# Experts' rooms by rank: 53 units of 128, 96, 64 and 32 places instead of 56 units

## The reference, cut to what matters

```python
def _moe(h, p):                                  # h: 384 x 1024
    ...                                          # top 8 of 64 experts for each token
    hg = jnp.einsum('td,edf->tef', h, p['w_gate'])      # 64 x 1024 x 128
    hu = jnp.einsum('td,edf->tef', h, p['w_up'])        # 64 x 1024 x 128
    act = jax.nn.silu(hg) * hu * gates[:, :, None].astype(h.dtype)
    routed = jnp.einsum('tef,efd->td', act, p['w_down'])   # 64 x 128 x 1024
    shared = (jax.nn.silu(h @ p['ws_gate']) * (h @ p['ws_up'])) @ p['ws_down']
    return routed + shared
```

## Time and profile before

| | |
|---|---|
| median of 3 runs | 1691.47 us (1687.89 to 1701.95) |
| profiled execution, its own time | 1706.42 us |
| its span, first to last instruction | 1704.6 us |
| PE busy | 1406.1 us, 82% of the span |
| DVE, ACT, POOL busy | 671.4, 408.3, 256.3 us |
| mean granted clock of PE | 0.881 of 2.4 GHz |
| moved by DMA | 378.96 MB, 222 GB/s over the span |
| chain that ended last | PE 71%, DVE 16%, DMA 6% |
| of it in the expert stage | L1143 25%, L1158 11%, L1129 7% |

### The profile page before, as it was taken

One profiled execution on the slowest core, in us unless ns is written; L12 is line 12 of the kernel. 1 busy time (PEld: TensorE's weight loads), 2 busy tenths in 40 slices (PEclk: granted clock), 3 DMA queues, 4 the chain that ended last, 5 costly groups with the idle time before them and its releaser, 6 DMA issues.

```text
span 1704.6 us, 23713 instructions
## 1 busy us (share of the span) xinstructions
PE 1406.1 (82%) x8772; PEld 962.6 (56%) x8772; DVE 671.4 (39%) x1382; ACT 408.3 (24%) x788; POOL 256.3 (15%) x273
## 2 busy tenths in 40 slices
PE   4799687986999999997059996888889999999942
PEld 2598465954555555554028875676655555555521
DVE  4422767153332222222743347633523222222246
ACT  2324425021222222221013344321112122222201
POOL 1000000001322222231010000000023232322200
PEclk9799857977999999999579996699889999999975
DMA  9553202126988888885874412122469888888853
GB/s 319 206 183 118 105 31 109 50 87 233 362 305 317 328 333 324 305 332 181 340 257 173 141 70 99 41 99 99 180 252 358 333 313 307 324 294 298 328 207 154
DMA packets 126098, 378.96 MB, mean 222 GB/s; under 512 B 28224, under 2 KB 33152, under 8 KB 122784
## 3 DMA queue, kind: packets, MB, share of 16 engines
q1 hardware_dynamic: 86976, 291.31, 46.2%
q0 software_dynamic: 35552, 60.97, 10.1%
q10 hardware_dynamic: 3456, 25.17, 3.6%
HBM read 480.36 MB, written 64.75 MB: 320 GB/s over the span
## 4 chain that ended last, share of the span: by engine, by line
PE 71%; DVE 16%; DMA 6%; issue 4%; ACT 2%; SPq 0%; DVEq 0%; ACTq 0%; POOLq 0%
PE bank L1143 25%; PE bank L1158 11%; PE bank L1129 7%; PE bank L1050 5%; PE bank L771 4%; PE bank L772 4%; PE bank L773 4%; DVE aT L1843 4%; DMA ring<-in_w_ada 3%; DVE aT L1580 1%; PE bank L1066 1%; DMA ring<-in_w_in 1%; PE bank L790 1%; PE bank L1114 1%; PE bank L976 1%
## 5 line engine op out<-in xcount | busy, mean ns | idle before, releaser
L1143 PE MATMUL bank<-slab,xT 128*64 128x256 f32 x2112 | 301.5, 396 | 20.6 <-issue 20.5
L1143 PEld LDWEIGHTS bank<-slab,xT 128*64 128x64 f32 x2112 | 180.6, 142 | 104.2 <-issue 38.2
L732 POOL DMA_INDIRECT sums_scratch<-h,row_table x112 | 112.8, 1007 | 538.6 <-PE bank L1129 438.4
L1826 DVE TENSOR_TENSOR work<-work,bank 128x128 f32<-128x128 f32 x112 | 32.3, 288 | 399.1 <-ACT work L1405 399.1
L1143 PE MATMUL bank<-ring,xT 128*64 128x256 f32 x960 | 152.7, 392 | 9.6 <-issue 9.6
L1158 PE MATMUL bank<-slab,work 128*64 128x512 f32 x528 | 147.3, 592 | 1.5 <-DVE work L1832 1.5
L1405 ACT ACTIVATE work<-bank 128x128 f32<-128x128 f32 x112 | 31.1, 278 | 457.5 <-PE bank L1143 457.5
L1815 DVE COPY h<-bank 128x512 f32<-128x512 f32 x112 | 77.5, 692 | 127.0 <-PE bank L1158 127.0
L1143 PEld LDWEIGHTS bank<-ring,xT 128*64 128x64 f32 x960 | 90.1, 140 | 44.8 <-issue 14.8
L1143 PE MATMUL bank<-h_hi_slot,xT 128*64 128x256 f32 x512 | 108.5, 396 | 6.4 <-issue 6.4
L1492 DVE TENSOR_TENSOR w_lo<-ring,w_hi 128x2048 fp32r<-128x2048 f32 x24 | 55.0, 2292 | 122.3 <-ACT w_hi L1229 122.3
(11 more groups left out here) (334 smaller groups left out, 2324.9 us busy)
## 6 DMA issues: line engine op xcount, KB each, us to landing
slab<-in_w_gate SPq DMA_DIRECT2D x112, 512.0 KB
slab<-in_w_up SPq DMA_DIRECT2D x112, 512.0 KB
slab<-in_w_down SPq DMA_DIRECT2D x112, 512.0 KB
ring<-in_w_ada SPq DMA_DIRECT2D x24, 2048.0 KB
ring<-in_w_gate SPq DMA_DIRECT2D x52, 512.0 KB
ring<-in_w_up SPq DMA_DIRECT2D x52, 512.0 KB
ring<-in_w_down SPq DMA_DIRECT2D x52, 512.0 KB
slab<-sums_scratch ACTq DMA_DIRECT2D x24, 1024.0 KB, 11.5
```

Source lines behind the costliest of these rows:

```text
L732: pool.indirect_dma_start(sums_dram, bass.IndirectOffsetOnAxis(ap=row_table[:, u:u + 1], axis=0), y_rows[:, n % 3, :], None, bounds_check= ...
L1143: last = mm(bk[r, 0:2 * P].rearrange("p (k f) -> p k f", k=2), xT[:, n % 2, j, r], w[:, j, :, :], start=(j == 0), stop=(j == NJ - 1))
```

## The change: rooms by rank, and products of the unit's own widths

There are 53 units. Ranks 0 to 7 have 128 places (8 units, kind "whole"); ranks 8 to 15 have 96, and share their unit with one of the ranks 56 to 63, which have 32 (8 units, "mixed"); ranks 16 to 47 have 64 (16 units, "pair"); ranks 48 to 55 have 32, four to a unit (2 units, "quad"); 19 units of two windows are spare. A turn is pair, whole, spare, pair, mixed, spare (the first: pair, whole, pair, mixed, spare, spare); turns 2 and 5 have a quad and a spare more, the last one a spare more.

A whole unit's products use 128 stationary columns, one product where two were. A mixed unit has three products of 64, 32 and 32 columns; a quad four of 32. The places and rooms come from a table by rank: constants that DVE builds at the start (`by_rank`), three products of it with a one-hot of the ranks (bank "rooms"), and a copy. The counts are divided into windows only after that, since the room is subtracted first. The 7 slots, L652 and the conditional loads stay as they are.

```diff
@@ -29,14 +29,15 @@
 BASE = 8
-LAYER_DVE = 159
+START_DVE = 29
+LAYER_DVE = 156
 NSLOT = 2
...
 WIN = 64
-NUNITS = 56
-WHOLE = 16
-PAIRED = 24
-NXW = 32
+NUNITS = 53
+BASE_UNITS = 34
+SPARE = NUNITS - BASE_UNITS
+NXW = 2 * SPARE
 EMPTY = 65536
...
@@ -46,6 +47,33 @@
               ("c_lat", 512), ("s_lat", 512), ("tie", 64))
+
+
+def windows_of(unit):
+
+    if unit < 8:
+        return [(0, P, unit)]
+    if unit < 16:
+        return [(0, 96, unit), (96, P, unit + 48)]
+    if unit < 32:
+        return [(0, WIN, unit), (WIN, P, unit + 16)]
+    if unit < BASE_UNITS:
+        return [(GROUP * k, GROUP * (k + 1), 48 + 2 * k + unit - 32) for k in range(4)]
+    return [(0, WIN, 64 + unit - BASE_UNITS), (WIN, P, 64 + unit - BASE_UNITS + SPARE)]
+
+
+def steps_by_rank(value, slope):
+    out = []
+    for r in range(1, len(value)):
+        if value[r] != value[r - 1] + slope:
+            out.append((r, value[r] - value[r - 1] - slope))
+    return out
+
+
+BY_RANK = sorted((r, unit * P + lo, hi - lo) for unit in range(BASE_UNITS) for lo, hi, r in windows_of(unit))
+PLACE_STEPS = steps_by_rank([place for _, place, _ in BY_RANK], P)
+ROOM_STEPS = steps_by_rank([room for _, _, room in BY_RANK], 0)
 
...
@@ -412,6 +444,7 @@
         banks.plan("layer", "ranks", 1, [7])
+        banks.plan("layer", "rooms", 1, [1])
         banks.plan("layer", "ysh", 2 * NTILE, [0, 1, 2, 3, 4, 5])
...
@@ -521,18 +554,22 @@
             landed.append(fix_sum[b % NSLOT])
-        UNITS_BY_KIND = {"whole": list(range(WHOLE)), "pair": list(range(WHOLE, WHOLE + PAIRED)),
-                         "spare": list(range(WHOLE + PAIRED, NUNITS))}
-        order_of_units = []
-        loads, loads_of_unit = [], []
+        UNITS_BY_KIND = {"whole": list(range(8)), "mixed": list(range(8, 16)), "pair": list(range(16, 32)),
+                         "quad": list(range(32, BASE_UNITS)), "spare": list(range(BASE_UNITS, NUNITS))}
+        order_of_units, loads, tiles_of_unit = [], [], []
         for turn in range(8):
-            for kind in ("pair", "whole", "pair", "spare", "pair", "whole", "spare"):
+            kinds = ("pair", "whole", "spare", "pair", "mixed", "spare") if turn > 0 else ("pair", "whole", "pair", "mixed", "spare", "spare")
+            for kind in kinds + {2: ("quad", "spare"), 5: ("quad", "spare"), 7: ("spare",)}.get(turn, ()):
                 u = UNITS_BY_KIND[kind].pop(0)
-                owners = {"whole": [u], "pair": [u, u + PAIRED], "spare": [E + u - WHOLE - PAIRED, E + u - WHOLE - PAIRED + 16]}[kind]
-                loads_of_unit.append([len(loads) + i for i in range(len(owners))] * (2 if kind == "whole" else 1))
-                loads += [(len(order_of_units), w) for w in owners]
+                tiles = []
+                for lo, hi, w in windows_of(u):
+                    cuts = [lo, 64, hi] if hi - lo == 96 else [lo, hi]
+                    tiles += [(slice(p, q), len(loads)) for p, q in zip(cuts, cuts[1:])]
+                    loads.append((len(order_of_units), w))
+                tiles_of_unit.append(tiles)
                 order_of_units.append(u)
-        assert sorted(order_of_units) == list(range(NUNITS)) and len(loads) == E + NXW
+        assert all(w < E for _, w in loads[:XSLOT])
+        assert sorted(order_of_units) == list(range(NUNITS)) and sorted(w for _, w in loads) == list(range(E + NXW))
 
...
@@ -1102,7 +1136,13 @@
                 banks.filled(mm(bk[:, 0:E], ones[0:E, :], is_less[0:E, :], start=True, stop=True), "ranks")
-                shared_up(1, range(2, NJ))
+                shared_up(1, range(2, 4))
+                bk = banks.claim(pe, "rooms")
+                banks.wait_emptied(pe, "ranks")
+                for k in range(3):
+                    last = mm(bk[:, k * E:(k + 1) * E], by_rank[:, k * P:(k + 1) * P], of_rank[0:E, :], start=True, stop=True)
+                banks.filled(last, "rooms")
+                shared_up(1, range(4, NJ))
                 bk = banks.claim(pe, "owner")
...
@@ -1130,16 +1170,15 @@
                 def up(n):
-                    for half in range(2):
-                        _, full, level = expert_slot(n, half)
+                    for i in sorted({i for _, i in tiles_of_unit[n]}):
+                        _, full, level = load_slot(i)
                         pe.wait_ge(full, level(l))
...
                     for j in range(NJ):
-                        for half in range(2):
-                            r = slice(WIN * half, WIN * (half + 1))
-                            w = expert_slot(n, half)[0][:, 0:2 * D].rearrange("p (k j f) -> p j k f", k=2, j=NJ)
+                        for r, i in tiles_of_unit[n]:
+                            w = load_slot(i)[0][:, 0:2 * D].rearrange("p (k j f) -> p j k f", k=2, j=NJ)
                             last = mm(bk[r, 0:2 * P].rearrange("p (k f) -> p k f", k=2), xT[:, n % 2, j, r], w[:, j, :, :],
...
@@ -1153,9 +1192,8 @@
                         bk = banks.claim(pe, stage, 0, n)
-                        for half in range(2):
-                            r = slice(WIN * half, WIN * (half + 1))
-                            last = mm(bk[r, :], actT[:, n % 2, r], expert_slot(n, half)[0][:, 2 * D + c * 512:2 * D + (c + 1) * 512],
+                        for r, i in tiles_of_unit[n]:
+                            last = mm(bk[r, :], actT[:, n % 2, r], load_slot(i)[0][:, 2 * D + c * 512:2 * D + (c + 1) * 512],
                                       start=True, stop=True)
...
@@ -1429,13 +1467,26 @@
             copy, red = nc.vector.tensor_copy, nc.vector.tensor_reduce
-            order = InOrder(dve, dve_order, 6, LAYER_DVE, DEPTH)
+            order = InOrder(dve, dve_order, START_DVE, LAYER_DVE, DEPTH)
             after = order.after
...
             dve.sem_inc(slots_idle.sem, 1)
+            dve.wait_ge(ids_ready, 1)
+            after(ts(rank_id[:, :], tie_col[:, :], -1.0, float(E - 1), ALU.mult, ALU.add))
+            ts(rank_col[:, 0:1], rank_id[:, :], float(P), None, ALU.mult)
+            after(nc.vector.memset(rank_col[:, 1:2], float(P)))
+            for k, steps in ((0, PLACE_STEPS), (1, ROOM_STEPS)):
+                for first, change in steps:
+                    after(ts(rank_step[:, :], rank_id[:, :], float(first), float(change), ALU.is_ge, ALU.mult))
+                    after(tt(rank_col[:, k:k + 1], rank_col[:, k:k + 1], rank_step[:, :], ALU.add))
+            after(tt(rank_col[:, 2:3], rank_col[:, 0:1], rank_col[:, 1:2], ALU.add))
+            after(ts(rank_col[:, 2:3], rank_col[:, 2:3], -1.0, float(BASE_UNITS * P), ALU.mult, ALU.add))
+            for k in range(3):
+                last = ts(by_rank[:, k * P:(k + 1) * P], ones[0:E, :], rank_col[:, k:k + 1], None, ALU.mult)
+            after(last)
             dve.wait_ge(consts_in, 16 * NCONST)
...
@@ -1729,38 +1780,33 @@
                 ts(is_less[0:E, :], key_row[0:E, :], key_col[0:E, :], None, ALU.is_lt).then_inc(less_ready.sem, 1)
-                copy(count_i, count)
-                after(ts(place_i[:, 0, :], loads_row, float(WIN - 1), None, ALU.add))
+
+                ranks = banks.read(dve, "ranks")
+                banks.emptied(ts(of_rank[0:E, :], ranks[0:E, 0:E], rank_id[:, :], None, ALU.is_equal), "ranks")
+                rooms = banks.read(dve, "rooms")
+                banks.emptied(copy(rstd[:, 2 * E:5 * E], rooms[:, 0:3 * E]), "rooms")
+                banks.wait_emptied(dve, "rooms")
+                tt(count_i, count, over_tiles_e(room), ALU.subtract)
+                after(stt(place_i[:, 0, :], loads_row, float(WIN - 1), room, ALU.add, ALU.subtract))
                 ts(count_i, count_i, 6, None, ALU.arith_shift_right)
...
                 copy(over_a[:, :, :], count_i)
-
-                ranks = banks.read(dve, "ranks")
-                after(ts(room, ranks[:, 0:E], float(WHOLE), None, ALU.is_lt))
-                ts(far, ranks[:, 0:E], float(WHOLE + PAIRED), float(WIN - PAIRED * P), ALU.is_ge, ALU.mult)
-                after(ts(room, room, 1.0, None, ALU.add))
-                banks.emptied(stt(own_place, ranks[:, 0:E], float(P), far, ALU.mult, ALU.add), "ranks")
-                after(tt(extra, place_i[:, 1, :], room, ALU.subtract))
-                after(ts(extra, extra, 0.0, None, ALU.max))
+                after(ts(extra, place_i[:, 1, :], 0.0, None, ALU.max))
                 after(nc.vector.tensor_tensor_scan(spans[:, 1, :], ones[:, 0:E], extra, 0.0, ALU.mult, ALU.add))
...
 
-                tt(over_base, spans[:, 0, :], room, ALU.subtract)
                 tt(own_span[0:E, :, :], spans[0:E, :, :], ident[0:E, 0:E].unsqueeze(1).broadcast_to([E, 2, E]), ALU.mult)
-                after(red(rank_col[0:E, :], is_less[0:E, :], AX.X, ALU.add))
+                after(red(rank_of[0:E, :], is_less[0:E, :], AX.X, ALU.add))
                 red(span_col[0:E, :], own_span[0:E, :, :], AX.X, ALU.add)
-                after(ts(rank_col[0:E, :], rank_col[0:E, :], -1.0, float(E - 1), ALU.mult, ALU.add))
```

(24 more changed lines are left out.)

## The result

| | before | after |
|---|---|---|
| median | 1693.8 us (4 runs) | 1908.8 us (4 runs, 1902.6 to 1915.2) |
| ratio | | 1.1266, 95% interval 1.1204 to 1.1328 |
| profiled execution, its span | 1706.4, 1704.6 us | 1907.8, 1906.0 us |
| expert stages, first to last unit's row | 378.6 and 382.1 us | 477.8 and 478.5 us |
| PE busy | 1406.1 us | 1509.3 us |

The account below looks back on a forecast made before the run. PE leads, busy over 95%, but not alone (DMA 83%), with waits for late weights. Stages +85.5 and routing +4.8 give +90.3 on the 1691.5 us median: 1782 us, range 1690 to 1895.

Parts of the forecast that it names:

- The step that failed: Products of mixed units: a 64-wide tile beside two 32-wide ones was taken to cost 0 us extra.
- The bound from above: Mixed units' up and down products, if both widths cannot run at once: 7.1 us more per unit.
- the sum: Whole kernel: +85.5 us in the expert stages and +4.8 us for routing, together +90.3 us.
- The rival's size: Mixed units' widths do not overlap: 56.8 us per layer, +46 after fewer waits, 1874 us in all; chance 0.27.
- The slots: Expert stages: order of loads against 7 slots makes weights late, 90 us of waits per layer; DMA share near 0.75.
- first pairs: First pairs of turns, units 6, 12, 26, 32, 46: last load's gate only three units earlier, late 2.2 us, five times.
- DMA volume: Rival for the expert stages: same bytes at share 0.83 take the same 380 us, 1696 us in all; chance 0.10.
- Three units less: Expert stages: three units go, at 6.456 us each, -19.4 us per layer.
- Routing: Ahead of the expert stage: DVE waits for small products, +2.7 less 0.3, +2.4 us per layer, +4.8 in all.
- Start: Kernel start: 26 new DVE operations end before 8 us while DVE idles until 13.48; 0 us.
- Full width: Whole units' products: one full-width product needs the same time as a pair; 0 us.
- Spare loads: Real spare windows in smaller rooms: one or two per layer possible, 0 to 5.3 us each; taken as 0.

Follow-up runs that it names:

- a_m32: Kernel after, with the 96-place window of each mixed unit cut into three 32-wide tiles, so all four tiles are 32 wide; 1801.4 us, ratio 1.0637.
- b_mix: Kernel before, with the second half of each of its 24 paired units cut into two 32-wide tiles beside the first half's 64; 2018.0 us.
- b_late: Kernel before, spare windows given a slot only when the unit three places ahead is through, real windows taking slots before; 1649.4 us, ratio 0.973.
- b_quart: Kernel before, with every paired unit done as four 32-wide tiles, loads and order untouched; 1696.6 us.
- a_halves: Kernel after, with whole units again done as two tiles of 64 columns; 1906.5 us.
- a_m32_late: Kernel after, mixed units in four 32-wide tiles, spare windows given slots only when the unit two places ahead is through; 1776.5 us.

## Why the prediction failed

- **The step that failed** is "Mixed units have a 64-wide tile beside two 32-wide ones, which no row shows ... I take 0, nearest to the two rows in which tiles do overlap". Both rows show tiles of one width. The bound from above was the truth: 7.1 us, measured 7.4 in the profile after (11.95 against 6.51 for unit 3, 8.55 against 6.59 for unit 5, after against a_m32) and 7.5 in b_mix. One step j of unit 10's up phase takes 1.13 us (496.67 to 497.80), where a step at one width takes 0.43 (794.34 to 794.77 in unit 55 of the kernel before). That is 2 x 0.43, the 64-wide tile and then the two 32-wide ones, and 0.27 more, about 0.14 for each of two changes of width, where I had taken 0.1. Two steps in the profile after, with the two 32-wide tiles of the first, which do run together (497.48 and 497.49), and one step of the kernel before:

```profile
496.67 0.98 PE L1182 MATMUL bank<-h_hi_slot,xT 128*64 128x256 f32 x3
497.48 0.38 PE L1182 MATMUL bank<-h_hi_slot,xT 128*32 128x256 f32 x1
497.49 0.38 PE L1182 MATMUL bank<-ring,xT 128*32 128x256 f32 x1
497.80 0.98 PE L1182 MATMUL bank<-h_hi_slot,xT 128*64 128x256 f32 x3
```

```profile
794.34 0.38 PE L1143 MATMUL bank<-slab,xT 128*64 128x256 f32 x1
...
794.77 0.38 PE L1143 MATMUL bank<-slab,xT 128*64 128x256 f32 x1
```

- The Trainium skill, TensorEngine Tiling (Array Packing), Tiling Modes, says that changing the tiling mode drains the engine, and lists 128x64 and 128x32 as different configurations. The trace agrees: 0 for four equal tiles in the up phase, 7.5 us for a mixture in b_mix.
- **What it weighs.** In spans the sum was 111.1 us short (201.4 against 90.3): 118.4 for 16 mixed units at 7.4, less 8.3, since the waits beside them were 85.5 and 86.2 us and not 90, and 1 for routing.
- **The rival's size.** With it I had 1874. In profiles it gives +182 against +201.4 measured. Of the difference, 5 us are 7.4 instead of 7.1, 12 are waits (I had taken 10.5 off 90.2 for each layer), about 1 is routing. Against the medians 13 us more are missing: the profiled execution of before ran 12.6 us over its median, those of the other kernels within 2, and I took its 55.7 us of waits for typical. Outside the stages it had 943.9 us, b_late 940.9 and b_quart 943.1, so most of the 13 us probably lay in the stages' own waits; no second trace of the kernel before shows it.
- **The slots: right**, in mechanism and size. Waits of 91.1 and 92.7 us in a_m32 for 90.2, and a DMA share of 0.74 and 0.72 for the 0.75 foretold. By kind, in its layer 0: unit 18 late by 14.3 (12.8 forecast), unit 20 by 10.6 (8.6), mixed units by 1.6 to 6.0, five of the seven by 4.2 or more (5.2), first pairs by 0.3 to 1.8 (2.2). That DMA volume isn't the limit is shown by b_late.
- **Three units less**: their 19.4 us per layer are in both sums. PE lost more in the eight mixtures, 59 us.
- **Routing: right.** From the ranks product to the maximum with zero there were 1.48 us (379.07 to 380.55 in the earlier trace rows); now 4.26. That is +2.8, forecast +2.7:

```profile
378.26 0.43 PE L1138 MATMUL bank<-norm_t,ones 64*128 64x64 f32 x2
...
380.11 0.88 PE L1143 MATMUL bank<-norm_t,by_rank 64*128 64x64 f32 x6
```

```profile
382.52 0.19 DVE L1794 TENSOR_SCALAR work<-work 128x64 f32<-128x64 int32 x1
```

- **Start: right.** The table is done at 6.3 us and DVE idles 7.37 us where it idled 12.43:

```profile
5.61 0.67 DVE L1488 TENSOR_SCALAR by_rank<-ones,rank_col 64x128 f32<-64x128 f32 x3
13.65 0.56 DVE L1491 CAST masks<-h 128x768 uint8<-128x768 f32 x1 [7.37 <-DMA lb_all<-in_lower_bounds]
```

- **Full width: right**, 0 (a_halves). **Spare loads: right** for the kernel after: one real window appeared, in layer 0, and its unit was in time.

## What to carry to other kernels

Rows of two tilings that each overlap say nothing about the two mixed: keep one tile width within a phase, even at the price of more products. A prefetch ring counts what is reserved, not what is fetched: give a slot to an optional transfer as late as its issue, done or not done, still lands in time, and check by walking the list which earlier unit each load waits for. When two resources are nearly in balance (64 loads of some 5.3 us, 340 us of DMA work, against 352 of PE here), the order of demands decides before either total does.

## What the runs showed of the hardware

Products 64 and 32 columns wide on different columns of the array run one after the other with about 0.14 us per change (1.13 us for a step of 2 x 0.43), while four of 32 or two of 64 run together: 64 products of 256 columns in 3.66 us, 32 in 3.67. A change of width between one unit and the next costs about as much: steps of 6.59 us in b_quart for 6.45. A conditional transfer that isn't carried out still takes 0.07 to 0.10 us on its queue, and a window of three, with the reading of its register, some 1.4 us (460.14 to 461.53 in a_m32_late). What waits for the window starts only then: 1.9 us late in 17 spare units of each layer there.
